# Scores of block 1's dilated attention by pairs of heads, and another order and another place for the subtraction in block 2's first attention

## The chip, the cores and the metric

One core of a Trainium2 chip runs the whole program. The metric is the device time in microseconds (us) of one execution; it is compared by the median of several. Engines that work in parallel and meet at semaphores: PE (TensorE, matrix products and transposes; weight loads are shown apart as PEld), DVE (VectorE), ACT (ScalarE), POOL (GpSimd) and SP (issues DMAs). Each engine runs its own list of instructions strictly in the order in which the program wrote them. PSUM has eight banks of 512 fp32 columns; PE writes there.

## The reference, cut to what matters

Two blocks, each of two layers, run one after the other on 512 tokens with a width of 1024, in fp32. The change touches two attentions. In block 1, in each of its two layers:

```python
# dilated_attention: 12 heads of 64 in three groups of four (dilation 1, 4, 16)
sc = einsum("bhqd,bhqkd->bhqk", qb[g], kk) * scale        # per group g
p = exp(sc - max(sc)); den = sum(p)
o = einsum("bhqk,bhqkd->bhqd", p, vv) / den
out = sum(softmax_over_groups(m + log(den)) * o)           # merged over the three groups
```

In block 2, in its first layer (512 tokens and 256 context tokens, 768 keys):

```python
# gqa_attend, 8 heads of 64: p = softmax(q k^T); o = p v
# diff_attend, 4 heads, each with two maps of 64 and values of 128:
s = einsum('bqhjd,bshjd->bhjqs', q, k); p = softmax(s)
a = p[:, :, 0] - lam * p[:, :, 1]
o = einsum('bhqs,bshe->bqhe', a, v)                         # then rms_norm per head
```

## The kernel before, in words

All tensors lie with channels on partitions and tokens on the free axis. Large products run as sums of three fp32r products (high part by high part, high by low, low by high): `products` (L582 to L588) issues three matmuls of 128x512 for each of eight blocks. Their weights stream in as units of 128x1024 that SP loads to `RAW`, ACT copies to the high part `WH` (`split_high`, L1314) and DVE turns into the low part `WL` (`split_low`, L1876). Smaller products in attention are plain fp32, and the trace shows each plain fp32 product as two matmul records (a transpose is one).

**Block 1.** After the projections, a loop over q = 0 to 23 on PE runs one unit of gate or branch weights per turn (`gate_unit`: 24 matmuls; `pool_and_conv_unit`, every third turn: 18) and weaves the attention into it. The attention has 16 steps per layer (one step is one half of a 128-row chunk, so one head's 64 rows, for one of four residues of the token number; `head`, `scores`, `transposed`, `values`). Turn q computes the scores of step q-1 ahead of the unit (3 products with 64 rows of contraction, L748), and in the middle of the unit the six transposes of step q-2 (L771) and the six value products of step q-3 (L757). DVE adds the mask and takes the maximum (`maxima_1`, L1866), ACT exponentiates in SBUF (L1482) and copies the transposed probabilities out of PSUM (L1488), DVE scales the output (L2111). Scores take banks 0 and 1, transposes banks 2 and 3, outputs bank 7.

**Block 2, layer 0** (`attention_full` on four engines). 48 pairs k: 24 plain ones (two heads each), then 24 of the differential heads (the two maps of one head). Six query blocks per chunk of 128 channels: four see all 768 keys ("full"), two see 256 ("short"). The scores of both members of a pair are fp32r products on the two halves of the rows (L1087), into banks 0 to 3, and wait for both exponentials of the pair before (`full_exp`). Then DVE takes the maximum of each (L2358), ACT exponentiates out of PSUM (L1644), DVE inverts the sum (L2364) and POOL writes a diagonal matrix with the inverse (`FULL_DIAG`, L534 and L536).
- Plain pairs: PE transposes the exponentials (L1109, three PSUM tiles of 512 columns: one per head, copied by ACT at L1650, and one shared, copied by DVE at L2371), multiplies with the values (L1148) and spreads the inverse over the partitions (`norms`, L1122), which ACT copies (L1674) and DVE multiplies onto the output (L2381). POOL splits that output (L524, L526).
- Differential pairs: PE multiplies the exponentials of both maps with their diagonals and adds them up in PSUM (L1111), the second diagonal carrying minus lambda; ACT takes the high part (`PTH`), DVE the low part (`PTL`, L2374), and the value product is three fp32r matmuls per key block for two pairs at once (L1152).

What sets the order is the code's own order: on each engine a loop over k issues the work of several pairs. On PE an iteration k is scores(k+1), norms(k-1), transposes of k, values of k-1. ACT in iteration k copies the norm of k-1, copies both transposed tiles of k (for differential pairs that of k-1), and only then exponentiates pair k+1.

## Time and profile before

| | |
|---|---|
| time, median of 3 executions | 3943.12 us (3937.47 to 4690.94) |
| time of the profiled execution | 3942.11 us |
| its span in the trace | 3940.3 us |
| PE matmul busy | 3719.2 us, 94% |
| PE weight loads busy (beside matmuls) | 3055.3 us, 78% |
| DVE busy | 2013.2 us, 51% |
| ACT busy | 1496.2 us, 38% |
| POOL busy | 257.4 us, 7% |
| chain that ended last | PE 82%, DVE 7%, ACT 6% |
| mean granted PE clock | 0.984 of full speed |

A matmul's duration in the trace includes its way through the array, so neighbouring matmuls overlap; what one costs is the distance from its start to the start of the next. The loops concerned: block 1's attention runs from 223.6 to 1372.9 us by its score rows (in two stretches, one per layer), block 2's first attention from 2250.8 to some 2487 us. A row names the engine, the kernel's line, what is written and read, and in brackets how long the engine had been idle before and what released it.

### The profile page before, as it was taken

The numbers are of one execution on the slowest core, as the hardware profiler recorded it, in microseconds if no ns is written. First come the engines' busy times: TensorE is split into PE (matmuls) and PEld (weight loads), VectorE is DVE, ScalarE is ACT, GpSimd is POOL, SyncE is SP. The second block draws the span as 40 slices with busy tenths as digits, with TensorE's granted clock in tenths as the row PEclk, the third lists the DMA queues.
The fourth block names the chain that finished last, engine by engine and source line by source line (L and its number), as shares of the span: only waits on it lengthen the run. The fifth ranks groups of instructions, "written<-read, shape, count | busy, mean of one in ns | idle before, by whom it ended". The sixth has DMA issues, their size and how long they took to land.

```text
span 3940.3 us, 53537 instructions
## 1 busy us (share of the span) xinstructions
PE 3719.2 (94%) x19778; PEld 3055.3 (78%) x19778; DVE 2013.2 (51%) x3431; ACT 1496.2 (38%) x2288; POOL 257.4 (7%) x412
## 2 busy tenths in 40 slices
PE   7999988999999999899989989989999988899997
PEld 5788876887787887688777768878888867677886
DVE  4633456777763355577764455353333253644443
ACT  4333355332323334533235256441222234753232
POOL 0000000000000000000000044000000001620000
PEclk9999999999999999999999999999999999999999
DMA  3212221445322122144541102111111112112221
GB/s 121 96 64 70 99 99 65 144 144 192 122 96 70 59 102 102 43 149 144 176 162 47 56 1 41 38 38 64 64 61 61 59 53 63 30 43 80 96 95 71
DMA packets 112433, 333.19 MB, mean 85 GB/s; under 512 B 32664, under 2 KB 33432, under 8 KB 111640
## 3 DMA queue, kind: packets, MB, share of 16 engines
q1 hardware_dynamic: 73472, 264.18, 19.2%
q0 software_dynamic: 14400, 52.44, 3.9%
q10 hardware_dynamic: 24408, 14.51, 1.6%
q8 instruction: 98, 1.61, 0.2%
q14 instruction: 55, 0.45, 0.0%
HBM read 328.99 MB, written 6.00 MB: 85 GB/s over the span
## 4 chain that ended last, share of the span: by engine, by line
PE 82%; DVE 7%; ACT 6%; issue 2%; DVEq 1%; DMA 1%; POOL 0%; ACTq 0%; POOLq 0%; SPq 0%
PE PS L586 13%; PE PS L588 13%; PE PS L587 13%; PE PS L959 10%; PE PS L962 10%; PE PS L960 10%; PE PS L661 2%; PE PS L748 2%; PE PS L1087 1%; PE PS L757 1%; PE PS L1111 1%; ACT PB L1644 1%; ACT L1350 1%; DVE Y L2332 1%; DVE HVAL L1920 1%
## 5 line engine op out<-in xcount | busy, mean ns | idle before, releaser
L1876 DVE TENSOR_TENSOR WL<-RAW,WH 128x1024 fp32r<-128x1024 f32 x494 | 604.2, 1223 | 520.0 <-ACT WH L1314 513.7
L1314 ACT ACTIVATE WH<-RAW 128x1024 fp32r<-128x1024 f32 x494 | 521.3, 1055 | 673.0 <-PE PS L962 363.4
L586 PE MATMUL PS<-HHI,WH 128*128 128x512 f32 x1632 | 649.5, 398 | 23.6 <-DVE HLO L1913 15.9
L588 PE MATMUL PS<-HHI,WL 128*128 128x512 f32 x1632 | 642.3, 394 | 0.0
L587 PE MATMUL PS<-HLO,WH 128*128 128x512 f32 x1632 | 638.0, 391 | 0.0
L959 PE MATMUL PS<-H2HI,WH 128*128 128x512 f32 (+1 forms) x1336 | 470.8, 352 | 0.0
L960 PE MATMUL PS<-H2LO,WH 128*128 128x512 f32 (+1 forms) x1336 | 445.3, 350 | 0.0
L586 PEld LDWEIGHTS PS<-HHI,WH 128*128 128x128 f32 x1632 | 307.3, 188 | 104.1 <-issue 23.0
L962 PE MATMUL PS<-H2HI,WL 128*128 128x512 f32 (+1 forms) x1336 | 387.9, 351 | 0.0
L588 PEld LDWEIGHTS PS<-HHI,WL 128*128 128x128 f32 x1632 | 307.2, 188 | 67.6
L587 PEld LDWEIGHTS PS<-HLO,WH 128*128 128x128 f32 x1632 | 307.4, 188 | 66.4 <-issue 0.5
L959 PEld LDWEIGHTS PS<-H2HI,WH 128*128 128x128 f32 x1336 | 251.0, 188 | 54.1 <-DVE WL L1876 0.3
L960 PEld LDWEIGHTS PS<-H2LO,WH 128*128 128x128 f32 x1336 | 250.8, 188 | 34.7
L959 PE MATMUL PS<-GHI,WH 128*128 128x512 f32 (+1 forms) x768 | 273.0, 355 | 0.0
L960 PE MATMUL PS<-GLO,WH 128*128 128x512 f32 (+1 forms) x768 | 260.1, 353 | 0.0
L962 PE MATMUL PS<-GHI,WL 128*128 128x512 f32 (+1 forms) x768 | 231.0, 355 | 0.0
L962 PEld LDWEIGHTS PS<-H2HI,WL 128*128 128x128 f32 x1336 | 215.8, 188 | 15.0
L2536 DVE TENSOR_TENSOR Y<-Y,PS 128x768 f32 (+1 forms) x64 | 52.5, 821 | 282.0 <-PE PS L962 282.0
L2521 DVE SCALAR_TENSOR_TENSOR TMP<-PS,TMP 128x768 f32<-128x768 f32 (+1 forms) x64 | 52.7, 824 | 248.8 <-ACT TMP L1836 248.8
L959 PEld LDWEIGHTS PS<-GHI,WH 128*128 128x128 f32 x768 | 144.3, 188 | 30.6
L661 PE MATMUL PS<-SQ,ONES 128*128 128x512 f32 (+1 forms) x256 | 111.4, 581 | 52.9 <-ACT SQ L1616 20.6
L960 PEld LDWEIGHTS PS<-GLO,WH 128*128 128x128 f32 x768 | 144.2, 188 | 21.3
(359 smaller groups left out, 5930.3 us busy)
## 6 DMA issues: line engine op xcount, KB each, us to landing
RAW<-in_stream SPq DMA_DIRECT2D x494, 512.0 KB, 3.2
MODW<-in_modw POOLq DMA_DIRECT2D x96, 512.0 KB, 3.6
bias_rows<-in_rpb ACTq DMA_DIRECT2D x8, 476.2 KB, 6.3
MEM<-in_mem ACTq DMA_DIRECT2D x3, 1024.0 KB, 4.7
X<-in_x SPq DMA_DIRECT2D x1, 2048.0 KB, 9.5
CROW<-in_crow POOLq DMA_DIRECT2D x4, 512.0 KB, 4.7
out<-X SPq DMA_DIRECT2D x1, 2048.0 KB, 7.0
BIAS<-bias_rows ACTq DMA_DIRECT2D x8, 224.0 KB, 4.5
```

Of the source, the lines that this page charges most:

```text
L586: nc.tensor.matmul(out, WH[:, slot, b * P:(b + 1) * P], hi, start=start, stop=False)
L587: nc.tensor.matmul(out, WH[:, slot, b * P:(b + 1) * P], lo, start=False, stop=False)
L588: return nc.tensor.matmul(out, WL[:, slot, b * P:(b + 1) * P], hi, start=False, stop=stop)
L661: last = nc.tensor.matmul(FLAT[:, 6 * T + c0:6 * T + c1], ONES[:], SQ[:, k % 2, c0:c1], start=k == 0, stop=k == KB - 1, skip_group_check=True)
L748: last = nc.tensor.matmul(o, q, k, start=True, stop=True)
L959: nc.tensor.matmul(o, WH[:, slot, w], hi[:, k, c], start=k == 0, stop=False, skip_group_check=True)
L960: nc.tensor.matmul(o, WH[:, slot, w], lo[:, k, c], start=False, stop=False, skip_group_check=True)
L962: last = nc.tensor.matmul(o, WL[:, slot, w], hi[:, k, c], start=False, stop=k == KB - 1, skip_group_check=True)
L1314: A(WH[:, d, :], RAW[:, s, :], ACT.Copy).then_inc(high_split, 1)
L1876: TT(WL[:, d, :], RAW[:, s, :], WH[:, d, :].bitcast(F32), ALU.subtract).then_inc(split_ready, 1)
L2521: STT(TMP[:, p, 0:n2], FLAT[:, 3 * p * T:3 * p * T + n2], 0.0, TMP[:, p, 0:n2], ALU.max, ALU.mult).then_inc(taken[p], 1)
L2536: TT(y, y, FLAT[:, 3 * p * T:3 * p * T + n2].unsqueeze(1), ALU.add).then_inc(taken[p], 1)
```

## The change

**Block 1.** Two steps (the two halves of the rows of one chunk) become one, on every second turn. On even turns PE issues the scores of both halves in alternation, into banks 0, 1 and 2, 3; on odd turns it transposes both into the same banks; on the next even turn come both value products. DVE, ACT and the semaphore counts follow. The counts of products, transposes and copies stay.

PE, block 1, two turns before (q = 8 and 9 or the like; gate and branch products left out by dots):

```order
L748 MATMUL PS<-U 128x512 [waits max_ready]
L748 MATMUL PS<-U 128x128 x2
...
L771 MATMUL PS<-IDENT,PB 128x128 [waits pts_ready,exp_done]
L771 MATMUL PS<-IDENT,PB 128x128 x5
L757 MATMUL PS<-U,PTS 128x64 [waits o_taken]
L757 MATMUL PS<-U,PTS 128x64 x5
```

And PE in two turns of the changed kernel (L751 are scores, L763 value products, L778 transposes):

```order
L751 MATMUL PS<-U 128x512 [waits pts_ready]
L751 MATMUL PS<-U 128x512
L751 MATMUL PS<-U 128x128 x4
...
L763 MATMUL PS<-U,PTS 128x64 x12
...
L778 MATMUL PS<-IDENT,PB 128x128 [waits exp_done]
L778 MATMUL PS<-IDENT,PB 128x128 x5
L778 MATMUL PS<-IDENT,PB 128x128 [waits exp_done]
L778 MATMUL PS<-IDENT,PB 128x128 x5
```

The first list stands once in every turn; the second is spread over two. The scores now wait for the copies of the transposed probabilities, since both use the same banks.

**Block 2, plain pairs.** On PE, norms move behind the values; on ACT, the copy of the second head's tile moves behind the exponentials, and the norm that is copied is that of k-2; DVE's output multiplication is that of k-2 and comes ahead of the maxima; POOL waits for `full_spread` before it overwrites a diagonal.

ACT in block 2, plain full pairs, before (L1674 norm, L1650 tile copies, L1644 exponentials):

```order
L1674 ACTIVATE FULL_NORM<-PS 128x128 [waits full_spread]
L1650 ACTIVATE PTF<-PS 128x4x128 [waits full_turned] x2
L1644 ACTIVATE FULL_P_137,DEN<-PS,MX 128x768 [waits full_max]
L1644 ACTIVATE FULL_P_138,DEN<-PS,MX 128x768 [waits full_max]
L1674 ACTIVATE FULL_NORM<-PS 128x128 [waits full_spread]
```

The same in the changed kernel (L1676, L1652, L1646):

```order
L1676 ACTIVATE FULL_NORM<-PS 128x128 [waits full_spread]
L1652 ACTIVATE PTF<-PS 128x4x128 [waits full_turned]
L1646 ACTIVATE FULL_P_137,DEN<-PS,MX 128x768 [waits full_max]
L1646 ACTIVATE FULL_P_138,DEN<-PS,MX 128x768 [waits full_max]
L1652 ACTIVATE PTF<-PS 128x4x128 [waits full_turned]
```

One of the two tile copies now stands behind the exponentials.

**Block 2, differential pairs.** DVE combines the two maps in SBUF (`combine`: the first map plus the second times minus lambda times the ratio of the sums, one 128x768 operation), PE multiplies that once with one diagonal, ACT copies it out after the exponentials, DVE takes no low part, and the value product is one plain fp32 product per block in place of three fp32r ones. The high and low parts of v are no longer made (four copies on ACT, four subtractions on POOL).

PE, differential pairs, before, in one iteration (eight diagonal products of a full pair, whose other four stand in the next iteration, and the first of three blocks of value products):

```order
L1087 MATMUL PS<-FULL_KH_150,U2R 128x256 x2
L1111 MATMUL PS<-FULL_DIAG,PB 128x128 [waits full_low,full_diag]
L1111 MATMUL PS<-FULL_DIAG,PB 128x128 x7
L1152 MATMUL PS<-PTH,FULL_VH_153 128x256
L1152 MATMUL PS<-PTL_136,FULL_VH_153 128x256
L1152 MATMUL PS<-PTH,U2R 128x256
```

And in the changed kernel (L1095 scores, L1123 diagonal products, L1155 all three blocks of value products):

```order
L1095 MATMUL PS<-FULL_KH_149,U2R 128x256 x2
L1123 MATMUL PS<-FULL_DIAG,FULL_COMB_153 128x128 [waits full_high,full_combined,full_diag]
L1123 MATMUL PS<-FULL_DIAG,FULL_COMB_153 128x128 x3
L1123 MATMUL PS<-FULL_DIAG,FULL_COMB_153 128x128 [waits full_high]
L1123 MATMUL PS<-FULL_DIAG,FULL_COMB_153 128x128
L1155 MATMUL PS<-PTF,U_119 128x256 x3
```

A full pair has six diagonal products now and had twelve, a block of values one product and had three, and PE waits for no low part.

The core of the diff:

```diff
-                def scores(n):
-                    jj, r, rows = head(n)
+                def scores(pair):
+                    jj, r = pair // 4, pair % 4
                     for g in range(3):
+                        for half in range(2):
+                            rows, b = slice(half * HD, half * HD + HD), 2 * half
...
-                    if q < 3:
-                        v_transposed(3 + q)
+                    if q == 0:
+                        v_transposed(3)
...
-                    elif 2 <= q <= 16:
-                        m.add("max")
-                        pe.wait_ge(max_ready, m.at("max"))
-                        scores(q - 1)
+                    if q % 2 == 0 and 2 <= q <= 16:
+                        if q >= 4:
+                            probs_in()
+                        scores(q // 2 - 1)
...
@@ attention_full, PE
-                            last = nc.tensor.matmul(FLAT[:, at:at + P], FULL_P[u.k % 2][h][:, c:c + P], FULL_DIAG[:, u.k % 2, h, :],
-                                                    start=adds is None or adds == 0, stop=adds is None or adds == 1, skip_group_check=True)
+                            last = nc.tensor.matmul(FLAT[:, at:at + P], FULL_COMB[u.k % 2][:, c:c + P], FULL_DIAG[:, u.k % 2, 0, :],
+                                                    start=True, stop=True, skip_group_check=True)
...
-                        for x, (lv, rp) in enumerate(((vh, PTH), (vh, ptl), (vl, PTH))):
-                            last = nc.tensor.matmul(PS[:, 7, 0:2 * P], lv[:, kb * P:(kb + 1) * P], rp[:, units[0].par, b, :, :].rearrange("p q n -> p (q n)"),
-                                                    start=b == blocks[0] and x == 0, stop=b == blocks[-1] and x == 2)
+                        last = nc.tensor.matmul(PS[:, 7, 0:2 * P], U2[:, V_CHUNK[j], kb * P:(kb + 1) * P],
+                                                PTF[:, units[0].par, b, :, :].rearrange("p q n -> p (q n)"), start=b == blocks[0], stop=b == blocks[-1])
...
-                    if 1 <= k <= 24:
-                        norms(k - 1)
...
                         values(k - 1, 1)
+                        norms(k - 1)
@@ attention_full, ACT
-                    if 0 <= k < FULL_PAIRS and plain(k):
-                        for n in TURNED_FROM[k]:
-                            if by_scalar(TURNED[n]):
-                                turned_high(n)
-                    if 24 < k <= FULL_PAIRS:
-                        turned_high(TURNED_FROM[k - 1][0])
+                    if halves:
+                        turned_high(halves[0])
                     if k + 1 < FULL_PAIRS:
                         exps(k + 1, 0)
                         exps(k + 1, 1)
...
+                    if halves:
+                        turned_high(halves[1])
+                    if 24 < k <= FULL_PAIRS:
+                        turned_high(TURNED_FROM[k - 1][0])
@@ attention_full, DVE
+                def combine(k):
+                    c = 5 + 2 * (k % 2)
+                    if k >= 26:
+                        dve.wait_ge(full_turned, TURNED_FROM[k - 2][0] + 1)
+                    n = TA if all_keys(k) else TC
+                    STT(FULL_COMB[k % 2][:, 0:n], FULL_P[k % 2][1][:, 0:n], MX[:, c:c + 1], FULL_P[k % 2][0][:, 0:n], ALU.mult, ALU.add).then_inc(full_combined, 1)
...
+                    if 2 <= k <= 25:
+                        output(k - 2)
+                    if k + 1 < FULL_PAIRS:
                         maximum(k + 1, 0)
                         maximum(k + 1, 1)
+                    if k >= 24:
+                        combine(k)
```

## Rows read from the trace of the kernel before

**Rows 1.** Busy us by engine in three stretches, then granted PE clock, DMA share, GB/s.

```profile
200.00:400.00 200.00, 200.00 (x971) 164.08 (x971) 73.45 (x160) 70.20 (x99) 0.00 (x0) 1.00 0.20 71
2259.00:2272.00 13.00, 11.40 (x62) 9.33 (x64) 5.32 (x9) 5.49 (x12) 1.81 (x3) 0.50 0.00 0
2380.00:2484.00 104.00, 95.57 (x820) 86.55 (x817) 54.58 (x115) 63.23 (x146) 40.85 (x57) 1.00 0.19 39
```

**Rows 2.** Timeline of PE in block 1: start, duration, line, count.

```profile
276.54 0.40 PE L588 MATMUL PS<-HHI,WL 128*128 128x512 f32 x1
276.86 2.16 PE L748 MATMUL PS<-U 64*128 64x512 f32 x6
278.96 0.50 PE L586 MATMUL PS<-HHI,WH 128*128 128x512 f32 x1
279.30 0.40 PE L587 MATMUL PS<-HLO,WH 128*128 128x512 f32 x1
```

**Rows 3.** The same scores in narrow windows: starts of second and third record.

```profile
277.52 1.04 PE L748 MATMUL PS<-U 64*128 64x512 f32 x3
...
277.95 0.85 PE L748 MATMUL PS<-U 64*128 64x128 f32 x3
```

**Rows 4.** Timeline of PE, value products of one step in block 1.

```profile
272.67 1.45 PE L757 MATMUL PS<-U,PTS 128*128 128x64 f32 x12
```

**Rows 5.** Timeline of DVE and ACT in block 1, first maximum and exponential.

```profile
260.96 0.69 DVE L1866 CUSTOM_DVE_ANT_0 PB<-PS,MASK 128x512 f32<-128x512 f32 x1 [4.54 <-PE PS L748]
...
262.54 0.94 ACT L1482 ACTIVATE PB<-PB,MX 128x768 f32<-128x768 f32 x1 [2.22 <-DVE MX L2104]
```

**Rows 6.** Timeline of one plain full iteration in block 2.

```profile
2327.91 0.50 PE L1087 MATMUL PS<-FULL_KH,FULL_QH 64*128 64x512 f32 x2 [1.48 <-ACT FULL_P L1644]
...
2329.16 0.44 PE L1122 MATMUL PS<-FULL_DIAG,ONES 128*64 128x128 f32 x4
...
2329.53 1.53 PE L1109 MATMUL PS<-IDENT,FULL_P 128*128 128x128 f32 x12
...
2330.22 1.08 ACT L1650 ACTIVATE PTF<-PS 128x512 f32<-128x512 f32 x2 [0.30 <-PE PS L1109]
2330.99 1.53 PE L1148 MATMUL PS<-PTF,U 128*64 128x128 f32 x24
...
2333.12 0.50 PE L1087 MATMUL PS<-FULL_KH,FULL_QH 64*128 64x512 f32 x2 [0.60 <-ACT PB L1644]
```

**Rows 7.** Timeline of PE: starts of the scores of plain pairs 18, 19 and 22.

```profile
2345.14 0.50 PE L1087 MATMUL PS<-FULL_KH,FULL_QH 64*128 64x512 f32 x2
...
2349.41 0.50 PE L1087 MATMUL PS<-FULL_KH,FULL_QH 64*128 64x512 f32 x2 [1.41 <-ACT PB L1644]
...
2365.03 0.39 PE L1087 MATMUL PS<-FULL_KH,FULL_QH 64*128 64x256 f32 x2 [0.60 <-ACT FULL_P L1644]
```

**Rows 8.** Timeline of the differential pairs: scores of pairs 36, 38, 39, 42.

```profile
2425.41 0.50 PE L1087 MATMUL PS<-FULL_KH,FULL_QH 64*128 64x512 f32 x2
...
2433.95 0.50 PE L1087 MATMUL PS<-FULL_KH,FULL_QH 64*128 64x512 f32 x2
...
2436.19 1.95 PE L1111 MATMUL PS<-FULL_DIAG,FULL_P 128*128 128x128 f32 x16
...
2437.09 0.89 ACT L1644 ACTIVATE PB<-PS,MX 128x768 f32<-128x768 f32 x1
...
2439.01 0.50 PE L1087 MATMUL PS<-FULL_KH,FULL_QH 64*128 64x512 f32 x2 [0.53 <-ACT PB L1644]
...
2452.18 0.50 PE L1087 MATMUL PS<-FULL_KH,FULL_QH 64*128 64x512 f32 x2
```

**Rows 9.** Timeline: POOL's first subtraction in block 2, and PE behind it.

```profile
2283.30 0.46 POOL L526 TENSOR_TENSOR H2LO<-FULL_O,H2HI 128x128 fp32r<-128x128 f32 x1 [8.34 <-issue]
...
2286.73 0.70 PE L1122 MATMUL PS<-FULL_DIAG,ONES 128*64 128x128 f32 x4 [4.11 <-POOL FULL_DIAG L534]
```

**Rows 10.** Groups by line and shape: a DVE operation of 128x768.

```profile
L2521 DVE SCALAR_TENSOR_TENSOR TMP<-PS,TMP 128x768 f32<-128x768 f32 x32 | 30.6, 957 | 161.4 <-ACT TMP L1836 161.4
```

More of the change, by code:

```diff
@@ L330, in by_vector @@
         def by_vector(u):
-            return not plain(u.k) or u.slots[1] - u.slots[0] == 2
+            return plain(u.k) and u.slots[1] - u.slots[0] == 2
         def scalar_count(n):
@@ L751, in values @@
-                def values(n):
-                    jj, r, rows = head(n)
-                    for b in range(6):
-                        g = max(b - 3, 0)
-                        vb = b if b < 4 else r
-                        v = U[:, C_V + 2 * g + jj, vb * P + rows.start:vb * P + rows.stop]
-                        last = nc.tensor.matmul(bank(7, HD), PTS[:, n % 2, b * P:(b + 1) * P], v, start=b == 0, stop=b == 5)
-                    last.then_inc(o_done, 1)
-                def probs_in(n):
-                    m.add("pts")
-                    pe.wait_ge(pts_ready, m.at("pts"))
@@ new lines, in values @@
+                def values(pair):
+                    jj, r = pair // 4, pair % 4
+                    for half in range(2):
+                        for b in range(6):
+                            g = max(b - 3, 0)
+                            vb = b if b < 4 else r
+                            v = U[:, C_V + 2 * g + jj, vb * P + half * HD:vb * P + (half + 1) * HD]
+                            last = nc.tensor.matmul(PS[:, 7, half * HD:(half + 1) * HD], PTS[:, half, b * P:(b + 1) * P], v, start=b == 0, stop=b == 5)
+                        last.then_inc(o_done, 1)
```

236 lines of the change are left out of this document (118 added, 118 removed).

## The prediction

> **What bounds the kernel now.** I read the busy times by stretch first, to see where PE is the bound. In block 1's attention PE is busy for 200.00 of 200 us at full clock, with DVE at 73 and ACT at 70 [rows 1]: there PE's own issue time is the time, and what PE no longer issues is gained. In block 2's first attention PE is not saturated: 95.57 of 104 us [rows 1]. There I read the timeline, iteration by iteration, for what the next scores wait for: it is always the exponential of the pair before (the brackets name ACT) [rows 6 to 8]. A matmul's duration overlaps its neighbour's, so I cost everything by distances between starts.
>
> **Block 1: scores by pairs.** Today one step costs PE this: the last product ahead of it starts at 276.54 and streams for 0.23 (the usual distance of such products: 279.30 is followed by one 0.23 later, and six of them make up the pace of the whole stretch), so PE is free at 276.77. The second record of the first product starts at 277.52, the third record at 277.95 [rows 3]; a record of 512 columns therefore takes 0.43, and the first must have streamed from 277.09, that is 0.32 after PE was free (a weight load that nothing hides). The four records of 128 columns take 0.22 each, to 278.84. The next unit starts at 278.96, but its second product comes 0.34 behind, 0.11 more than usual [rows 2], so the unit is in fact under way at 279.07. One step: 279.07 - 276.77 = 2.30; two steps: 4.60.
>
> Each product uses half of PE's rows. In the changed order the two halves follow one another, and the question is whether their records overlap. For fp32r scores in block 2 they do: the row at 2327.91 counts two products of 512 columns that start together [rows 6]. For plain fp32, with two records per product, the nearest case is the value product of block 2, whose two heads take different halves of the columns: 24 records in 1.53 [rows 6], against 12 records in 1.45 where nothing can overlap [rows 4]. So records pair up, and I lay them out in order: half 0's first record of 512 columns, then its second beside half 1's first, then half 1's second: 3 x 0.43 = 1.29; the eight of 128 columns that follow take four more slots of 0.22 = 0.88. With 0.32 to enter and 0.23 to leave: 2.72. Gain per pair 4.60 - 2.72 = 1.88; 8 pairs in each of two layers: 16 x 1.88 = **30.1 us**. Bounds: if the weight loads of the halves cannot run side by side, twelve loads of 0.22 and 0.55 around them give 3.2 and a gain of 22; full overlap, 2.30 per pair, gives 37. I take the middle one, since the column case overlaps in full.
>
> What must hold for this: nothing else may take PE's place. (a) The scores now wait for both copies of the transposed probabilities. They are made in the second half of the odd turn, which lasts 9 x 0.23 = 2.1 us at least; the second copy ends about 1.0 behind the last transpose (0.8 for a copy of 768 columns, 0.2 to start), so 1.1 us stay. (b) DVE does two chains of maxima in a row; one takes 262.54 - 260.96 = 1.58 [rows 5], the pair 3.2. Behind them `split_low` stands (1.22 in the page's groups), whose weights PE needs one unit later: scores 2.7, then 18 products (4.1) and both heads' value products (2.5) = 9.3 after the turn's start, and DVE is done at 2.5 + 3.2 + 1.2 = 6.9. 2.4 us stay. (c) The exponentials are read in the next turn's middle; late by nothing.
>
> Here a page bears on the size. The Trainium skill, "TensorE: Matmul & The Clock Gate", section on packing small matmuls, measures 3.07x for four row tiles, not 4x. An estimate by its efficiency (0.77, so 1.53x for two) makes the streaming part 3.48 / 1.53 = 2.3 in place of my 2.17, and the gain some 2 us smaller. The trace bears on the same matter with 24 records against 12 [rows 4, 6], close to twofold.
>
> **Block 2, plain pairs.** A full iteration lasts 5.21 [rows 6]. PE: scores 1.25, norms 0.37, transposes 1.46, values 1.53, then 0.60 idle for the exponential: 4.61 of work. ACT: the transposes start 1.62 behind the scores, the first tile copy 0.69 behind that, two copies take 0.97, then both exponentials (1.93 to the next scores): 1.62 + 0.69 + 0.97 + 1.93 = 5.21, which closes. The change takes the norms from ahead of the transposes (0.37) and one copy from ahead of the exponentials (0.49): ACT's chain falls to 4.35, at which PE is nearly the bound (4.61, less 0.1 for one change between array layouts that falls away). So 4.5 where a full pair's transposes and values meet, 4.35 where the values are of a short pair. Three of six iterations are of the 5.21 kind (2349.41 to 2365.03 is 15.62) [rows 7]; the one before is undisturbed at 4.27 and stays so, as do the two short ones, in which PE's work is the bound already. Per group of six: 0.86 + 0.71 + 0.71 = 2.3; three steady groups: **6.8 us**. The moved DVE output multiplication stands ahead of the maxima now; it waits for a norm that PE issued before the scores and ACT copies in 0.3, so it ends near 1.0, and the maxima could not start before 1.35: hidden, by 0.3 us. If that cover went, each full iteration would lose what is over.
>
> The first group is special. POOL's first subtraction hangs for 8.34 us, and PE then waits 4.11 for a diagonal [rows 9], in a stretch that had half a clock shortly before [rows 1]. The hang comes again. But norms now stand behind values, so PE does some 2 us of transposes and values under it, and POOL reaches it some 1.4 us earlier. I count 4.5 here, 0.9 for the first copy that is no longer ahead of the exponentials at half clock, and 0.2 for the rest; **5.6 us**, between 0 and 9.
>
> **Block 2, differential pairs.** A group of six takes 2452.18 - 2425.41 = 26.77; two of its full iterations last 5.07 (2433.95 to 2439.01) [rows 8]. In these the exponential starts at 3.14 and not at the undisturbed 2.34, behind the copy of products that PE had to finish first (24 records at 0.11 = 2.7 per pair). With half the products, and the copy behind the exponentials, the chain is the undisturbed 4.27 [rows 7]. PE's work: scores 1.25, 12 records 1.35, values. A value block of 256 columns in plain fp32 is two records of half of 0.43 [rows 3], so 0.43 against 3 x 0.12 before: dearer by 0.07, three blocks 1.3. Sum 3.9: under 4.27. In a short iteration PE issues 0.56 + 1.35 + 1.3 + 0.1 = 3.3, above its chain. Group: 4 x 4.27 + 2 x 3.3 = 23.7, gain 3.1; four groups **12.3 us**. The new DVE operation costs some 0.96 (a two-tensor one of 768 columns) [rows 10], from 3.2 (end of the maxima) to 4.1 of each iteration; PE needs it at 5.5: 1.4 to spare.
>
> A rule that speaks against this edit: the Trainium skill, "SBUF — State Buffer", section on the two sides, says that a VectorE operation with two SBUF inputs and a GpSimd one that reads SBUF exclude each other for a whole instruction. No row here has the pair. By it the combination would now and then stand behind a POOL subtraction; that would use up the 1.4 spare and cost, as an estimate, some 1 to 3 us over eight places.
>
> **The sum**, against the profiled execution's own 3942.1 us (1.0 under the median of the runs): 3942.1 - 30.1 - 6.8 - 5.6 - 12.3 = **3887**. The tail of the stage (table load, last copies) I cost at nothing: the copy behind the table load comes later by about what the missing low parts give back.
>
> **Rivals.**
> 1. *Halves do not overlap for two-record fp32.* Then a pair saves only one entry and one exit, 0.55: 9 us. 3942 - 9 - 24.7 = 3908. For it: no fp32 row with row halves exists; against it the column case. 0.12.
> 2. *Block 2 does not do what it says*: another wait (norm, output, combination) takes the place of the copy and iterations keep 5.2 and 5.1. 3942 - 30 = 3912. For it: five semaphore edges are new, and the cover of the output is 0.3 us. 0.13.
> 3. *A wait in block 1*, (a) or (b) above: each us beyond the spare costs 16. With 1 us: 3903. 0.07.
> 4. *More than I count*, full overlap and the hang hidden: 3942 - 37 - 33 = 3872. 0.10.
> 5. *Slower: the clock.* PE idles more in block 2, and after idling it ran at 0.50 for 13 us [rows 1]. At half clock PE's work of a plain group (22 us) is 44 against 26.7 now, +17; of a differential one (18.3) 37 against 26.8, +10. From about four of the seven groups on it outweighs the rest; all seven: 3942 - 30 + 51 + 40 - 6 = 3997. Against it: the clock is 1.00 over all of 2380 to 2484 with PE idle in every iteration [rows 1]. 0.03.
> The forecast itself, 3875 to 3900, keeps 0.55.
>
> **Range and chances.** 3866 to 3916 takes in rivals 1 to 4 and their bounds. A change of 2% (79 us), about the least that a measurement of this kernel can tell, lies at 3864: all cases but the ends are within it, though all but one are on the faster side. Faster 0.05, same 0.93, slower 0.02.
>
> **What would show it.** Block 1: twelve score records per pair with pairs of them starting together, some 2.2 us long, no idle PE, and the time between first and last scores of a layer shorter by 15. Plain iterations of 4.3 to 4.6; differential full ones of 4.27, short ones of 3.3. Wrong if score records follow one another at 0.43, if brackets of PE name `PTS` copies or weights in block 1, if iterations of block 2 wait for a norm, a diagonal or a combination, or if the granted clock falls there.

## The result and the profile after

The changed kernel takes 3876.87 us, median of 4 executions (3874.77 to 3882.91), the kernel before beside it 3942.61 (4 executions, 3937.47 to 4690.94). The ratio is 0.984, 95% interval 0.9821 to 0.9859: 1.6% faster, less than the 2% by which a change of this kernel counts as told apart, and 10 us below the forecast of 3887. (The execution of 4690.94 us is a slow one of the kernel before and is left out of the ratio.) The profiled execution took 3882.91 us with a span of 3881.1.

The busy times of the page, whole program (engine, us, share of the span, instructions):

```profile
PE 3661.7 (94%) x19498; PEld 3006.7 (77%) x19498; DVE 2014.7 (52%) x3415; ACT 1489.6 (38%) x2284; POOL 241.6 (6%) x384
```

PE lost 57.5 us of busy time, and the span 59.2. To see where, I matched the same instruction in both traces (VectorE's subtraction that makes low parts, which stands at the same places in both programs) and compared starts. Relative to the kernel before, the changed one gains 17.6 us between such places around layer 1's part of block 1's attention, 18.0 around layer 2's, and 26.8 around block 2's first attention; that is 62.4. The other 3.2 are lost and won elsewhere by amounts that differ from profile to profile (4 us of them within the first 100 us, ahead of all that was changed).

**Block 1.** The timeline of PE in the stretch that answers to [rows 2], the scores of a pair and the unit behind them:

```profile
280.66 0.40 PE L592 MATMUL PS<-HHI,WL 128*128 128x512 f32 x1
280.99 2.18 PE L751 MATMUL PS<-U 64*128 64x512 f32 x12
283.10 0.50 PE L590 MATMUL PS<-BHI,WH 128*128 128x512 f32 x1
283.44 0.39 PE L591 MATMUL PS<-BLO,WH 128*128 128x512 f32 x1
```

Twelve records last 2.18 us where six lasted 2.16: the second half costs nothing. Two narrow windows into it (281.15 to 281.50, then 281.66 to 281.90) name the records under way in each:

```profile
280.99 0.82 PE L751 MATMUL PS<-U 64*128 64x512 f32 x2
...
280.99 1.25 PE L751 MATMUL PS<-U 64*128 64x512 f32 x4
```

In the first window two records are under way, which start together at 280.99; in the second, four. From the previous product (280.66) to the next unit (283.10) it is 2.44 us, where [rows 2] has 2.42 for one step. Read as the prediction read one step (free 0.23 behind the previous product, and the unit under way 0.23 ahead of its second product at 283.44), a pair costs 283.21 - 280.89 = 2.32, about the 2.33 of the experiments below. PE stays busy for 199.19 of 200 us there:

```profile
200.00:400.00 200.00, 199.19 (x1047) 165.78 (x1046) 83.16 (x174) 77.22 (x113) 0.00 (x0) 1.00 0.23 77
2226.00:2236.00 10.00, 9.26 (x73) 7.87 (x74) 5.03 (x10) 6.40 (x14) 1.94 (x4) 0.67 0.00 0
2367.00:2391.00 24.00, 20.00 (x147) 15.99 (x147) 16.34 (x31) 16.09 (x38) 7.64 (x9) 1.00 0.31 62
```

(These are windows, in the columns of [rows 1]; the second and third belong to block 2 below.)

**Block 2, plain pairs.** The timeline of the full iteration that answers to [rows 6]:

```profile
2277.89 0.50 PE L1095 MATMUL PS<-FULL_KH,FULL_QH 64*128 64x512 f32 x2 [1.56 <-ACT PB L1646]
...
2279.14 1.53 PE L1121 MATMUL PS<-IDENT,PB 128*128 128x128 f32 x12
...
2279.83 0.60 ACT L1652 ACTIVATE PTF<-PS 128x512 f32<-128x512 f32 x1 [1.82 <-PE PS L1121]
2280.32 0.89 ACT L1646 ACTIVATE FULL_P<-PS,MX 128x768 f32<-128x768 f32 x1
2280.60 0.66 PE L1152 MATMUL PS<-PTF,U 128*64 128x128 f32 x8
...
2281.09 0.39 PE L1132 MATMUL PS<-FULL_DIAG,ONES 128*64 128x128 f32 x4
...
2282.08 0.60 ACT L1652 ACTIVATE PTF<-PS 128x512 f32<-128x512 f32 x1
...
2282.24 0.50 PE L1095 MATMUL PS<-FULL_KH,FULL_QH 64*128 64x512 f32 x2 [0.77 <-ACT FULL_P L1646]
```

The transposes now begin 1.25 behind the scores (1.62 before), one copy of 0.6 stands ahead of the exponentials, the other behind them, and the iteration lasts 4.35 us for 5.21.

**Block 2, differential pairs.** The full iteration that answers to [rows 8]:

```profile
2378.12 0.50 PE L1095 MATMUL PS<-FULL_KH,FULL_QH 64*128 64x512 f32 x2 [1.01 <-ACT FULL_P L1646]
...
2379.37 1.60 PE L1123 MATMUL PS<-FULL_DIAG,FULL_COMB 128*128 128x128 f32 x12
2379.47 1.82 DVE L2366 TENSOR_REDUCE MX<-PS 128x1 f32<-128x768 f32 x2 [0.80 <-PE PS L1095]
2380.46 0.90 ACT L1646 ACTIVATE PB<-PS,MX 128x768 f32<-128x768 f32 x1 [1.57 <-DVE MX L2366]
...
2381.21 1.01 DVE L2390 SCALAR_TENSOR_TENSOR FULL_COMB<-FULL_P,MX,FULL_P 128x768 f32<-128x768 f32 x1
...
2382.39 0.49 PE L1095 MATMUL PS<-FULL_KH,FULL_QH 64*128 64x512 f32 x2 [0.99 <-ACT PB L1646]
```

In the kernel before, the copy that stood directly ahead of the exponential (2437.09 in [rows 8]) waited for PE's products:

```profile
2436.39 0.81 ACT L1650 ACTIVATE PTH<-PS 128x768 fp32r<-128x768 f32 x1 [1.67 <-PE PS L1111]
```

Now the exponential starts 2.34 behind the scores (3.14 before), released by the maximum and no longer by PE, and the iteration lasts 4.27. PE is idle for 1.0 us of it: the chain scores, maximum, two exponentials is now the limit.

The distances between starts of scores, in us, with those of the kernel before (a group is six query blocks, four with all keys and two with a third of them):

| | before | after |
|---|---|---|
| first plain group | 8.07, 6.64, 7.46, 5.20, 3.84, 9.16 = 40.37 | 8.08, 5.78, 5.99, 4.38, 3.69, 6.36 = 34.27 |
| steady plain group | 4.27, 5.21, 5.21, 5.21, 3.84, 2.97 = 26.70 | 4.27, 4.35, 4.39, 4.51, 3.69, 2.81 = 24.02 |
| steady differential group | 4.25, 4.30, 5.07, 5.07, 4.49, 3.61 = 26.77 | 4.27, 4.27, 4.27, 4.27, 3.38, 3.38 = 23.84 |

The first group has two places of its own, which answer to [rows 9]. GpSimd stands still again for 8.34 us, and PE waits 1.97 behind it (before: 4.11), through the output multiplication on VectorE that waits for GpSimd:

```profile
2245.28 0.46 POOL L529 TENSOR_TENSOR H2LO<-FULL_O,H2HI 128x128 fp32r<-128x128 f32 x1 [8.34 <-issue]
...
2245.87 0.29 DVE L2403 TENSOR_TENSOR FULL_O<-PS,FULL_NORM 128x128 f32<-128x128 f32 x1 [3.48 <-POOL H2LO L529]
2246.31 2.83 PE L1152 MATMUL PS<-PTF,U 128*64 128x128 f32 x24 [1.97 <-DVE FULL_O L2403]
```

And from 2226 to 2236 the granted clock is 0.67 in the mean (window above): up to some 2232.5 it is 0.50 (1.2 GHz), behind that 1.00 (2.4 GHz). Earlier PE had waited 6.76 us for the exponentials of the pair before, ahead of the scores at 2223.29. The third iteration, from 2229.08, takes 5.99 us.

### The profile page after: what moved, and what is told of

Its sections match the earlier page's. It is cut to its first block, busy times and chain, and to the rows that moved or that the text cites. A ratio compares the mean times of both kernels' runs of the same rounds, so it can differ in the third digit from the quotient of the medians.

```text
span 3881.1 us, 52985 instructions
## 1 busy us (share of the span) xinstructions
PE 3661.7 (94%) x19498; PEld 3006.7 (77%) x19498; DVE 2014.7 (52%) x3415; ACT 1489.6 (38%) x2284; POOL 241.6 (6%) x384
## 4 chain that ended last, share of the span: by engine, by line
PE 82%; DVE 7%; ACT 6%; issue 2%; DVEq 1%; DMA 0%; POOL 0%; ACTq 0%; POOLq 0%; SPq 0%
PE PS L590 13%; PE PS L591 13%; PE PS L592 13%; PE PS L967 10%; PE PS L968 10%; PE PS L970 10%; PE PS L665 2%; PE PS L1095 1%; PE PS L763 1%; PE PS L751 1%; ACT FULL_P L1646 1%; ACT PB L1646 1%; ACT L1349 1%; DVE Y L2340 1%; DVE MX L2366 1%
## 5 line engine op out<-in xcount | busy, mean ns | idle before, releaser
L665 PE MATMUL PS<-SQ,ONES 128*128 128x512 f32 (+1 forms) x256 | 115.2, 601 | 49.4 <-ACT SQ L1618 19.5
```

Source lines behind the costliest of these rows:

```text
L665: last = nc.tensor.matmul(FLAT[:, 6 * T + c0:6 * T + c1], ONES[:], SQ[:, k % 2, c0:c1], start=k == 0, stop=k == KB - 1, skip_group_check=True)
```

## Experiments

**Each block's part alone.** Two kernels, each with one half of the diff.

> Only block 1's part of the change, block 2 as before. The trace of the changed kernel shows a pair's scores at 2.33 us between the units (2.10 from the first record to the next unit) where two steps took 4.60, and each of the two attention stretches shorter by some 17.8 us. Theory (both halves run fully beside one another, nothing new waits): 35 to 36 us faster than before, span by some 36. Rival (the parts help or hinder one another, for instance by the time at which the weights arrive): a gain clearly off 36, with the rest of the 62 to 66 us not explained by the other part alone.

> Only block 2's part of the change, block 1 as before. From the traces, block 2's first attention lasts 26.8 us less. Theory: 26 to 27 us faster, with iterations of plain full pairs of 4.3 to 4.5, differential full 4.27 and short 3.4 us, as in the changed kernel. Rival: another share. With e1 the sum should be 62 to 63.

Block 1's part: 3905.59 us (4 executions, 3898.69 to 3907.09), ratio 0.9908 (0.9891 to 0.9924); by the matched instructions 17.6 us in layer 1 and 18.0 in layer 2, as with the whole change. Block 2's part: 3916.36 (3912.57 to 3920.15), ratio 0.9936 (0.992 to 0.9953); 25.9 us in the attention, for 26.8. The kernel before took 3941.73 beside them. By the medians the parts are worth 36.1 and 25.4 us, together 61.5, and by the matched instructions 35.6 and 25.9, also 61.5, where the whole change has 62.4 in its profile. Within that the parts add up; a part of one or two us that one takes from the other could not be seen.

**Why a pair costs 2.33 and not 2.72: the order of the records.** The same twelve score records, but half by half:

```
-                    for g in range(3):
-                        for half in range(2):
+                    for half in range(2):
+                        for g in range(3):
```

> The changed kernel with block 1's scores issued half by half (three products of the upper rows, then three of the lower) in place of alternating. If PE sends records strictly in the order of the program, as the prediction assumed, only the last record of the first half and the first of the second can overlap: some 3.6 us per pair and 16 x 1.3 = 20 us slower than the changed kernel. If each half of the rows has its own line of work and PE looks far enough ahead, the pair stays at 2.33 us and the time of the changed kernel. Between these: PE looks ahead by a few records only.

3892.41 us in one execution, between the two outcomes named; 9.8 us gained in each layer where the alternating order gains 17.6 and 18.0. The pair in PE's timeline, and two narrow windows in it, 281.15 to 281.50 and 280.60 to 281.70:

```profile
280.52 3.25 PE L751 MATMUL PS<-U 64*128 64x512 f32 x12
283.70 0.50 PE L590 MATMUL PS<-BHI,WH 128*128 128x512 f32 x1
...
280.52 1.24 PE L751 MATMUL PS<-U 64*128 64x512 f32 x2
...
280.52 1.91 PE L751 MATMUL PS<-U 64*128 64x512 f32 x4
```

Six records last 2.16 by themselves [rows 2], so in 3.25 us the second half's series starts 1.09 behind the first's. In the first window only two records are under way, the first at 280.52 and another behind it, where the alternating order had two that started together. The second half enters about when the first's two records of 512 columns have gone in (0.66 and 0.43), and from then on both run side by side. The second window bears this out: up to 281.70 only four records have begun, and the last of them ends at 282.43, 0.82 behind 281.61, as long as the first record of a half lasts (0.82 in the alternating order; a record of 128 columns takes about half of that). So the second half's first record starts at 281.61, ahead of the first half's last three, which stand before it in the program. The strict order of the prediction, in which it could only have overlapped the sixth record (3.6 us per pair), is refuted; that PE finds the second half wherever it stands is refuted too. Alternation is what makes the second half free. Why a record six places behind starts beside the third and not beside the first stays open. (Which half a record belongs to is not in the rows; it is worked out from the lengths.)

**The order on ScalarE, put back.** The changed kernel with the second tile copy of plain iterations, and the tile copy of differential ones, ahead of the exponentials:

```
                         turned_high(halves[0])
+                        turned_high(halves[1])
+                    if 24 < k <= FULL_PAIRS:
+                        turned_high(TURNED_FROM[k - 1][0])
                     if k + 1 < FULL_PAIRS:
                         exps(k + 1, 0)
                         exps(k + 1, 1)
-                    if halves:
-                        turned_high(halves[1])
-                    if 24 < k <= FULL_PAIRS:
-                        turned_high(TURNED_FROM[k - 1][0])
```

> The changed kernel, but ScalarE makes the second tile copy of a plain iteration and the tile copy of a differential iteration ahead of the exponentials again, as before the change. Everything else, the products by halves and the one diagonal per differential iteration too, stays. Theory (the order on ScalarE carries most of block 2's gain; the products by halves are a smaller part): the long iterations come back nearly whole, a plain full one to 4.7 to 5.1 us where the changed kernel shows 4.27 to 4.51 and the kernel before 5.21, a differential full one to 4.9 to 5.1 where the changed kernel shows 4.27; a plain group of six takes about 26.0 us instead of 24.0, and the span is longer than the changed kernel's by 12 to 20 us. Rival (the order of the copies is free, because TensorE has other work to do until the exponentials come; the gain is the saved TensorE work alone): the periods stay at 4.3 and the span within 3 us of the changed kernel's.

3914.19 us in one execution, 37 us above the changed kernel where 12 to 20 were expected; block 2's first attention takes 4 us more than in the kernel before. Plain group: 4.27, 4.84, 4.85, 4.85, 3.69, 2.81 = 25.31. The full iterations are within what was expected, the group is 0.7 below it. The order of the one copy is worth 1.3 us of the group's 2.7; the rest is left to the norms and the shorter chain around them, which no run takes apart. Differential group, from the 36th query block: 4.24, 4.27, 5.51, 7.09, 5.29, 4.06. The full iterations were expected at 5.1 and are far above. The timeline of one shows why:

```profile
2370.84 0.81 ACT L1652 ACTIVATE PTF<-PS 128x768 f32<-128x768 f32 x1 [2.20 <-PE PS L1123]
2371.55 0.90 ACT L1646 ACTIVATE FULL_P<-PS,MX 128x768 f32<-128x768 f32 x1
...
2373.47 0.38 PE L1095 MATMUL PS<-FULL_KH,FULL_QH 64*128 64x256 f32 x2 [2.23 <-ACT FULL_P L1646]
...
2374.10 2.93 PE L1123 MATMUL PS<-FULL_DIAG,FULL_COMB 128*128 128x128 f32 x12
```

ScalarE waits for the products before it copies, copies for 0.7, and only then come the exponentials; PE waits 2.23 for them. These 5.51 are the order alone, for the granted clock is 1.00 (2.4 GHz) up to this point. Behind it PE's next twelve products take 2.93 us instead of 1.60, at a clock of 0.50 (1.2 GHz):

```profile
2350.00:2373.80 23.80, 16.75 (x124) 13.36 (x126) 13.32 (x24) 13.48 (x32) 4.49 (x6) 1.00 0.24 50
2374.00:2377.20 3.20, 3.20 (x15) 3.06 (x14) 3.02 (x4) 0.83 (x2) 2.31 (x2) 0.50 0.52 79
```

The mean is 0.86, 0.93, 0.85 and 0.87 in four windows between 2343 and 2440, where the changed kernel has 1.00. Three of the full iterations last 6.88 to 7.09 instead of 5.51, and VectorE's combination took 1.92 to 2.60 us instead of 1.01 in three places (more of this below). Part of the price of the wrong order is thus clock, and rival 5 of the prediction is real one step away from this kernel; how the rest of the loss divides was not taken apart.

**The order alone, in the kernel before.** Differential copies behind the exponentials, both heads still combined on TensorE:

```
-                    if 24 < k <= FULL_PAIRS:
-                        turned_high(TURNED_FROM[k - 1][0])
+                    if 24 < k < FULL_PAIRS:
+                        act.wait_ge(full_turned, TURNED_FROM[k - 1][0] + 1)
                     if k + 1 < FULL_PAIRS:
...
+                    if 24 < k <= FULL_PAIRS:
+                        turned_high(TURNED_FROM[k - 1][0])
```

The added wait is one that the copy had made until then: TensorE's products read the very tiles into which the exponentials write.

> The kernel before, with one thing of the change: in the differential iterations the tile copy of ScalarE stands behind the exponentials. The differential heads are still combined on TensorE, with both diagonals. Theory (two things are worth something in the differential part, the order on ScalarE and the work taken off TensorE): the full iterations go from 5.07 us to 4.4 to 4.6, and the group of six from 26.77 to 24.6 to 25.4, short of the changed kernel's 23.84; the short ones of 3.61 and 4.49 stay within 0.1. Over the 18 iterations that is 4 to 6 us off the span. Rival A (the order gives all of it): the group takes 23.8 us, as in the changed kernel, and the span falls by 9. Rival B (the work on TensorE gives all of it): the group stays at 26.8 and the span too.

3952.88 us in one execution: none of the three. A differential group takes 4.33, 4.99, 4.47, 5.12, 5.60, 3.60 = 28.11, 1.3 more than in the kernel before; the attention loses 7.2 us. In its timeline:

```profile
2445.60 1.13 PE L1111 MATMUL PS<-FULL_DIAG,FULL_P 128*128 128x128 f32 x8 [0.35 <-DVE PTL L2376]
2446.70 2.05 PE L1111 MATMUL PS<-FULL_DIAG,PB 128*128 128x128 f32 x16
2446.77 0.90 ACT L1644 ACTIVATE FULL_P<-PS,MX 128x768 f32<-128x768 f32 x1 [1.57 <-PE PS L1111]
```

The exponential still waits for PE's products (1.57), and now PE waits for the low part that VectorE makes from the late copy. Without the combined tile the order gains nothing; it moves the wait on.

**The combined tile without its release.** The changed kernel, with only the wait back that the kernel before could not do without:

```
+                    if 24 < k < FULL_PAIRS:
+                        act.wait_ge(full_turned, TURNED_FROM[k - 1][0] + 1)
                     if k + 1 < FULL_PAIRS:
                         exps(k + 1, 0)
```

> The changed kernel with one wait more: in the differential iterations the exponentials of the next query block start only once TensorE has finished the transposing products of the one before, as they had to in the kernel before, where the products read the tiles that the exponentials write. Nothing is taken away. Theory (the combined tile sets the tiles of the exponentials free earlier, and this is part of the gain): the exponentials start at the end of the products, 2.85 us behind the start of the scores instead of 2.34, and a full iteration goes from 4.27 to 4.75 to 4.85 us; a group of six takes 25.5 to 26.0 us instead of 23.84 and the attention 5 to 6 us more. Rival (the exponentials never get there before the products are done in a way that counts; the shorter products alone make the gain): 4.27 stays, and the group is within 0.3 us of 23.84.

3885.80 us beside 3876.93 for the changed kernel on that chip. The group: 4.32, 4.32, 4.83, 4.81, 3.38, 3.38 = 25.04 for 23.84, and the attention gains 19.5 us where it gained 28.8. The iteration in the timeline:

```profile
2380.23 0.49 PE L1095 MATMUL PS<-FULL_KH,FULL_QH 64*128 64x512 f32 x2 [1.07 <-ACT FULL_P L1646]
...
2381.47 1.60 PE L1123 MATMUL PS<-FULL_DIAG,FULL_COMB 128*128 128x128 f32 x12
...
2383.11 0.90 ACT L1646 ACTIVATE PB<-PS,MX 128x768 f32<-128x768 f32 x1 [2.11 <-PE PS L1123]
...
2385.04 0.50 PE L1095 MATMUL PS<-FULL_KH,FULL_QH 64*128 64x512 f32 x2 [1.53 <-ACT PB L1646]
```

The exponential starts at the products' end, 2.88 behind the scores. Two of the four full iterations pay 0.55 as expected, the other two, which follow the short blocks, 0.05. The group is shorter than the 25.5 to 26.0 expected, since only two iterations of it pay, and the attention loses more than the 5 to 6 us expected. Three groups account for 3.6 us of the 9.3; 3.7 more go at the first two long differential iterations (6.39 and 6.15 us for 4.56 and 4.26, with a granted clock of 0.79 between 2334 and 2342), and the other 2 behind the last scores. So the differential part of the change rests on several things at once: the copy behind the exponentials (0.69 per long iteration: 5.51 with copies first against 4.82 here), the exponentials' tiles free when VectorE has combined them, not when TensorE has read them (0.55), and the work taken off TensorE and VectorE (half the products, no low part), whose share no run has alone.

**GpSimd's 8.34 us.** What does it stand still for? Three kernels do some of its operations once, ahead of the loop, some 240 us earlier: the subtraction alone; the converting copy, a drain and the subtraction; the converting copy and the drain alone.

```
+            nc.gpsimd.tensor_copy(FULL_NORM[:, 0, :].bitcast(F32R), IDENT[:])
+            pool.drain()
+            nc.gpsimd.tensor_tensor(FULL_NORM[:, 1, :].bitcast(F32R), IDENT[:], FULL_NORM[:, 0, :], ALU.subtract)
             for k in range(FULL_PAIRS + 2):
```

> The changed kernel with one more POOL subtraction of 128x128 long before block 2's attention, while POOL is idle. Theory: the 8.3 us in which POOL's first subtraction hangs belong to the first use of that kind of instruction; they move to where nobody waits, the scores of pairs 5 to 6 come 2.8 to 3.7 us apart instead of 6.36, the stretch at half clock behind shrinks, and the kernel gets 3 to 5 us faster than the changed one. Rival: the hang belongs to the place (the drain ahead of it, or what lies between), stays where it is, and the time stays.

> The changed kernel, with GpSimd's pair of a converting copy and a subtraction, 128x128 each with the drain between them, done once ahead of its loop of block 2's first attention, some 240 us before their first use there; the values are not used. An earlier subtraction of the same size by itself did not take away the 8.34 us in which GpSimd stands still between the first converting copy and its subtraction. Theory (the stillness belongs to the first use of the converting copy, or of the sequence): it moves to the new place, where nothing waits for GpSimd, and the first use in the attention runs in 1.2 us; the first group of six plain scores, 34.27 us in the changed kernel, shortens by 2 to 5 us, and the kernel is faster than the changed kernel by as much: 3872 to 3875 us. Rival (it belongs to the place in the program, for instance to instructions that have to be fetched there): 8.34 us are still there, and the time is the changed kernel's within 2 us. A middle case: it moves but the first group is held by something else, and the time doesn't change.

> The changed kernel with only the converting copy of 128x128 and the drain ahead of GpSimd's loop, and no subtraction. Theory A (the stillness of 8.34 us belongs to the first converting copy): it is gone from the attention, and the first group takes 29.2 us, as with both operations. Theory B (it belongs to the first subtraction that writes the type of 32 bits which TensorE reads, whatever stands ahead of it): 8.34 us are still there between the two, and the group takes 34.3.

With the subtraction alone (3879.91 us, 3874.89 to 3882.70 in 4 executions) the 8.34 us stayed. With both operations they moved to the new place, where nobody waits; the timeline of GpSimd in that kernel, run again on another chip:

```profile
1995.90 0.84 POOL L531 CAST FULL_NORM<-IDENT 128x128 fp32r<-128x128 f32 x1
2005.16 0.45 POOL L533 TENSOR_TENSOR FULL_NORM<-IDENT,FULL_NORM 128x128 fp32r<-128x128 f32 x1 [8.42 <-issue]
...
2234.46 0.46 POOL L529 TENSOR_TENSOR H2LO<-FULL_O,H2HI 128x128 fp32r<-128x128 f32 x1
```

With the converting copy and the drain alone (3877.55 us in one execution) they are gone from the attention too (the subtraction at 2236.68 has no wait in its row). So the stillness doesn't belong to the subtraction. It belongs to the first converting copy of the program or to the first drain on GpSimd: in every kernel here the drain stands right behind that copy, the kernel with the subtraction alone had neither ahead of the loop, and no run has one without the other. The last distance of the first group, which the stillness had lengthened, is 5.97 to 6.36 us in the seven profiles of kernels that have it there and the new order of copies, and 2.81, 2.82 and 2.82 in the three that don't: 3.2 to 3.5 us.

Is that a faster kernel? Both ran in five rounds on one chip.

> The changed kernel itself, run beside the next one on the same chip. Theory: 3872 to 3883 us, 0.982 to 0.986 of the kernel before; the first group of six plain scores takes 34.3 us in its profile, with GpSimd standing still for 8.34 us in it.

> The same kernel as e8: the changed kernel with GpSimd's converting copy and its subtraction done once ahead of the loop. Theory: the 5.0 us that the first group lost less in e8 (29.24 instead of 34.27) are there in the time too, 3 to 7 us below the changed kernel on the same chip. Rival: the group is shorter again, but the time isn't, because something behind the attention gives it back: within 1.5 us of the changed kernel.

The changed kernel: 3876.93 us (3876.71 to 3877.33); with the early copy and subtraction: 3877.45 (3869.07 to 3883.72), and 3876.15 (3871.42 to 3880.62) in the batch before, where 3872 to 3875 was expected. The attention gained 28.8 and 30.4 us in the two profiles, and 32.0 in the earlier one. The wait is gone in every trace, but the total doesn't show it: its executions scatter by 14.7 us, and a gain of 3 cannot be told in that. It stays open whether something takes it back.

The other 1.6 to 1.8 us between profiles are the third distance of the first group: 4.37 to 4.39 us in the four profiles with a granted clock of 1.00 over that iteration, and 5.97 to 6.22 in the six with 0.68 to 0.71. The same program falls on one side or the other: the changed kernel has 5.99 in its first profile and 4.38 in the second, so that its first group took 32.45 there and not the 34.3 expected.

**VectorE against GpSimd.** In the changed kernel the timeline has both engines' operations longer than elsewhere in three places, the first and longest of which is:

```profile
2340.30 1.01 DVE L2390 SCALAR_TENSOR_TENSOR FULL_COMB<-FULL_P,MX,FULL_P 128x768 f32<-128x768 f32 x1
2340.44 2.56 POOL L520 TENSOR_TENSOR U2R<-U,FULL_KH 128x768 fp32r<-128x768 f32 x1 [0.43 <-ACT FULL_KH L1640]
2341.39 0.17 DVE L2379 RECIPROCAL MX<-DEN 128x2 f32<-128x2 f32 x1
2341.65 1.36 DVE L2381 SCALAR_TENSOR_TENSOR MX<-MX,LM,DEN 128x1 f32<-128x1 f32 x1
```

The subtraction takes 1.81 elsewhere, the operation on one column (L2381) 0.22. The other two places have 2.00 and 0.81 at 2364.82, and 2.01 and 0.81 at 2388.67. To make such meetings frequent:

```
+                    if 30 <= k < 42:
+                        pool.drain()
+                        nc.gpsimd.tensor_tensor(FULL_KH[0], U2[:, 17, :], U2[:, 17, :], ALU.subtract)
```

> The changed kernel, with one more subtraction of 128x768 on GpSimd in each of twelve differential iterations (the 31st to the 42nd), which writes a tile that nothing reads any more. Theory (while a VectorE operation reads two tiles of SBUF and GpSimd works, one of them stands still): subtractions that fall together with VectorE's combination of the two tiles take 2.3 to 2.9 us instead of 1.81, or small VectorE operations of 0.22 us take 1 us and more; since the diagonals of the next iteration stand behind the subtraction on GpSimd, the full iterations go from 4.27 to 4.4 to 5.0 us, and the twelve together cost 1 to 8 us. Rival (no such conflict; what was seen once was another wait): all subtractions take 1.8 us, VectorE's operations keep their times, and the periods stay at 4.27 and 3.38 within 0.05.

3883.46 us in one execution. The groups of the stretch, by form (first GpSimd from 2350 to 2420, then VectorE from 2366 to 2415):

```profile
L543 POOL TENSOR_TENSOR FULL_KH<-U 128x768 fp32r<-128x768 f32 x12 | 17.6, 1466 | 2.0 <-issue 2.0
...
L520 POOL TENSOR_TENSOR U2R<-U,FULL_KH 128x768 fp32r<-128x768 f32 x2 | 5.1, 2528 | 0.0
...
L2393 DVE SCALAR_TENSOR_TENSOR FULL_COMB<-FULL_P,MX,FULL_P 128x768 f32<-128x768 f32 x5 | 7.4, 1477 | 0.0
L2384 DVE SCALAR_TENSOR_TENSOR MX<-MX,LM,DEN 128x1 f32<-128x1 f32 x13 | 5.5, 421 | 1.5 <-issue 0.4
L2393 DVE SCALAR_TENSOR_TENSOR FULL_COMB<-PB,MX 128x768 f32<-128x768 f32 x4 | 5.2, 1296 | 0.0
L2393 DVE SCALAR_TENSOR_TENSOR FULL_COMB<-PB,MX 128x256 f32<-128x256 f32 x2 | 3.5, 1729 | 0.0
```

VectorE's combination takes 1.48 and 1.30 us in the mean instead of 1.01, the one of 256 columns 1.73 instead of 0.48; the kernel's own subtraction for the keys 2.53. The short iterations go from 3.38 to 3.79 to 3.89. Of the eight full ones only one gets longer (4.51); 4.4 to 5.0 had been expected for all of them, and they keep 4.25 to 4.29. Together it is 2.1 us over the twelve, within the 1 to 8 expected. The extra subtractions themselves took 1.47, not the 1.8 or more expected; they read one tile twice. The reciprocal, also on SBUF, kept its 0.17. The Trainium skill, "SBUF — State Buffer", section on the two sides, says that a VectorE operation with two inputs in SBUF and a GpSimd operation that reads SBUF exclude each other, and that the one that starts first shuts the other out for its whole length. The trace agrees for VectorE's operations of two inputs. The longest one is in the timeline of the kernel with copies first:

```profile
2405.31 1.81 POOL L520 TENSOR_TENSOR U2R<-U,FULL_KH 128x768 fp32r<-128x768 f32 x1 [0.28 <-ACT FULL_KH L1640]
2405.32 2.60 DVE L2389 SCALAR_TENSOR_TENSOR FULL_COMB<-FULL_P,MX,FULL_P 128x768 f32<-128x768 f32 x1
```

Both start together; GpSimd keeps its 1.81 us, and VectorE's 1.01 become 2.60, nearly the sum of the two.

## Why the prediction was right, and where it was not

The total was 10 us too high; by the stretches of the profile the kernel gained 62.4 us where the sum had 54.8. The forecast fell within its range; two of its terms were too small (1 and 2), and a third came near only because two errors in it made up for each other (3).

1. *Block 1, 30.1 predicted, 35.6 measured.* The time per step, 2.30, and the argument that nothing takes PE's place were right: no unit there waits for copies, maxima or low parts. The step that failed is "so records pair up, and I lay them out in order", which put half 0's second record beside half 1's first and made the pair 2.72. The two halves run side by side from the first record; a pair costs 4.60 - 35.6/16 = 2.37, within 0.05 of the 2.33 read in the timeline. The bound of full overlap (37) was the case, named with rival 4. I had laid the order out as if a half could start only one record later, and took no row that spoke for it: the row at 2327.91 [rows 6], where two products of one record each start together, spoke against it. The sign that I named, a row of twelve records some 2.2 us long, came true by luck: the single half's row is already 2.16 long, and by my own layout the pair's would have been some 2.6. The Trainium skill, "TensorE: Matmul & The Clock Gate", section on packing small matmuls, has 3.07x for four row tiles; the estimate by it would have made the gain smaller still. For two tiles in alternation these runs show two for one.
2. *Plain full iterations, 4.35 to 4.5: 4.35, 4.39, 4.51.* The chain on ScalarE and its two shortened links were right, and the long one is long because PE's work is the bound there, as argued. The short iterations were costed at no change and got 0.15 shorter each; that this is the one change of array layout that falls away is my reading, no run shows it alone. A steady group gained 2.7 for 2.3, the three groups 3.15, 2.67 and 2.70, together 8.5 for 6.8. The norm and the output multiplication, whose cover was 0.3 us, hold nothing up.
3. *First plain group, 5.6 predicted, 6.1 measured, with other parts.* At the place of the hang 2.8 us were gained, not 4.5: the output multiplication on VectorE, which I had moved ahead of the maxima, waits 3.48 for GpSimd, and PE for it, a path that I had not followed past the diagonal. The five other distances gave 3.3 instead of 1.1. That the sum of the two is near is luck.
4. *Differential pairs, 12.3 predicted, 12.2 measured* (26.8 less the 14.6 of the plain pairs; 11.3 of it by the starts of scores, the other 0.9 behind the last ones, where I had costed nothing). Full ones 4.27 as predicted, short ones 3.38 for 3.3, group 23.84 for 23.7. What the argument did not say, and the experiments show, is that no one edit has this gain: with the copy in front it is lost and more, and with the old tiles' release a group loses 1.2 of its 2.9 us.
5. *Contention with GpSimd* was given 1 to 3 us in a sentence beside the sum, and nothing in the sum. It happens (in three places, at most 2.56 and 1.36 us), and costs nothing that shows: it falls into short iterations, which last 3.37 to 3.39 us like the others. The combination itself is not held up there, so the 1.4 us to spare were not put to the test.
6. *Rivals.* Halves that don't overlap, a failing block 2 and a wait in block 1 are refuted by the rows above. The clock (rival 5) is not refuted but small here: 1.6 us in the first group, 0.3 at the start of the differential pairs (1.0 in the kernel with block 2's part alone). In the kernel with copies first, with PE idle for 2.2 us per iteration, it came with three full iterations that were 1.4 to 1.6 us longer.

## What to carry over

Where two matmuls use different halves of the rows, issue them in alternation: record by record the second was free here, half by half it cost 1.1 us of 2.2. In a ring of engines, count what an instruction ahead of the critical one costs (a copy of 0.8 cost 0.69 of each long iteration), and what the tile that it writes must wait for; a copy or a combination that sets that tile free earlier can be worth nearly as much as the order (0.55). Try such edits together: the late copy alone only moved the wait here, and made the attention 7 us longer.

## What was unexpected

Two-record fp32 products on two halves run fully side by side: 2.18 us for twelve records against 2.16 for six, and 3.25 in the other order. A record of the second half starts ahead of three that stand before it in the program. GpSimd stands still for 8.3 to 8.4 us behind its first converting copy and the drain that follows it, and an earlier subtraction doesn't take that away. In the loop that leaves PE idle for 1.0 us per iteration the granted clock stayed at 1.00; in the one with 2.2 us it was 0.85 to 0.93 in the mean, with 2.93 us at 1.2 GHz for products of 1.60. A VectorE operation of 1.01 us took 2.60 beside one of GpSimd.
